# One layer of a hybrid encoder: parts of the FFN fronts, the projection's start, the scan's copies and the first output product moved to other places

## The chip, the cores and the metric

One core of one Trainium2 chip runs the whole layer as one program. The metric is the device time of one execution in microseconds (us), median of several executions. The engines are TensorE (PE, with its weight load PEld), VectorE (DVE), ScalarE (ACT), GpSimd (POOL) and SyncE (SP, which here only issues transfers). Each engine runs its own instructions in program order; semaphores order them against each other.

## What is computed

The reference is one layer on 1024 positions of width 1024 in float32, cut here to what matters.

```python
h = x
h = h + 0.5 * swiglu(rmsnorm(h, ffn1_norm), w_gate1, w_up1, w_down1)     # d_ff 2816
n = rmsnorm(h, mix_norm)
z = n @ w_in     # -> c_q 256 | c_kv 128 | k_rope 32 | u 512 | gate_attn 1024 | gate_ssm 1024
q  = rmsnorm(c_q, q_norm) @ w_uq         # 8 heads, 64 + 32 (rotary)
kv = rmsnorm(c_kv, kv_norm) @ w_ukv      # 8 heads, keys 64, values 64
attn = softmax(q k^T / sqrt(96)) v       # bidirectional, 8 heads
y = S5_forward(u) + S5_backward(u) + D*u # complex diagonal state, 32 groups, 64 states
g = gelu(y) @ w_glu + b_glu
ssm = g[:512] * sigmoid(g[512:])
h = h + (sigmoid(gate_attn) * (attn @ w_o_attn) + sigmoid(gate_ssm) * (ssm @ w_o_ssm)) @ w_out
h = h + 0.5 * swiglu(rmsnorm(h, ffn2_norm), w_gate2, w_up2, w_down2)
out = rmsnorm(h, final_norm)
```

## The kernel before

**Arithmetic.** Every float32 product is made of three passes on reduced operands: each operand is split in a high part (`hi`, a cast on ACT) and a rest (`lo`, a subtraction on DVE or POOL), and `three_passes` (L46) issues hi·hi, hi·lo and lo·hi into one PSUM tile (L48 to L50). So each operand tile goes raw, `high` (ACT), `low` (DVE or POOL), PE.

**Phases.** The program is a row of phases with a barrier of all engines between them (L69 is the instruction on which they wait): `ffn_phase` "f1", `project_phase`, `ssm_phase`, `mixer_phase`, `merge_phase`, `ffn_phase` "f2". `rows` holds the residual stream in SBUF, 8 tiles of 128 positions (ST = 8); KT = 8 slices of the width.

**FFN.** `ffn_phase` multiplies with seven products for each 2x2 block (A is the weight side, B the token side), q = 0 to 6. Blocks that are sums (`S`, made by `sums` on POOL, L1300) feed q = 1 and the other summed ones. At its front the eight tiles of `rows` are squared (L898, ACT), normalised in groups of two (`squares`, `normalised`; `Rstd`, L361), scaled (L1052, DVE), combined on POOL (L1282 to L1287) and turned on PE (L1314); `lows` are tiles 4 to 7, `sums` the combinations. The products begin in the order (block 0, q 0), (0, 2), (1, 0), (1, 2), then (0, 1), (0, 3) and so on; (0, 1) needs all four turned sums (`sums_high`, `sums_low`) and the operand `A_hi`, `A_lo` of block 1 (L933, L1036). In f2 the first raw weights and the gain are loaded by the merge before it; squares of tiles 0 to 3 are made there too.

**Projection.** `Norm` (L269) normalises and turns `rows` into `nT_hi`, `nT_lo`. Tiles 4 to 7 were scaled at the end of f1 and are turned at once, tiles 0 to 3 are squared, scaled (`pjn_xn`, L309) and turned after. `RowProduct` (L190, tag `rp`) then multiplies by 16 units of weights (two jobs of 448 and 512 columns, 8 slices each), with two weight slots: load, `high` (ACT, L230), `low` (DVE, L240), and 24 matmuls on PE over the 8 tiles of rows.

**SSM.** DVE runs a scan of 127 steps of three small operations (L1758, L1760, L1762). Beside it PE makes gate products: `Gates` (L1553, tag `ga`), one for each of 16 columns of 128, with two weight slots and two PSUM slots. For product n ACT reads the PSUM result of n with `sigmoid(n)` (L1587), which frees that slot for product n + 2, and then issues `high(n + 2)`; POOL makes `low(n + 2)` (L173). 13 products stand before the first output block (GATES_FIRST = 13), three between the blocks. `forward(b)` (L1703) copies the scan's states `ss_H` into `rows` with two copies on ACT (L1711); `forward(0)` waits for the semaphore of the last step of the scan (`act.wait_ge(s["scan"], CH)`). The output blocks on PE (L1683) wait for the copies.

**Mixer and merge.** The mixer makes the product with `w_glu` (`glu`, N = 8 products), turns the latents (`latent(m)`, 8 of them, one after each glu product), projects keys and queries of head 0 (`project(0, x)`), makes the product with `w_o_ssm` (`wos`, KT = 8) with one `value(m)` after each, and then the attention. The merge begins with `woa` (the product with `w_o_attn`, columns 0 to 7; the weights of the first 3 are loaded and split before), adds `gate` and `part` to it (L2466, L2469), multiplies by `w_out` and adds to `rows`, which it loads back as one transfer of 4 MB (`rows<-kept`, L2416). At the end f2 stores `rows` tile by tile to `kept` before it scales them.

Of the kernel before, what the change touches and what calls it, by code (L numbers as in the profile page):

```python
# [14 lines left out]
F32 = mybir.dt.float32  # L15
# [174 lines left out]
class RowProduct:  # L190

    def __init__(self, nc, ctx, tag, jobs, lhs, psum):
# [4 lines left out]
        self.raw = [sb(f"raw{i}", [P, HALF]) for i in range(2)]  # L199
        self.hi = sb("hi", [P, 2, HALF], F32R)  # L200
        self.lo = sb("lo", [P, 2, HALF], F32R)
        self.raw_in = [sem(f"raw_in{i}") for i in range(2)]
# [5 lines left out]
    def load(self, sp, n):  # L208
        units = self.units()
        w, parts, width = self.jobs[units[n][0]]  # L210
        k = units[n][1]
        if n >= 2:
            sp.wait_ge(self.lo_done, n - 1)
        for at, cols in parts:
            sp.dma_start(self.raw[n % 2][:, at:at + cols.stop - cols.start], w[k * P:(k + 1) * P, cols]).then_inc(self.raw_in[n % 2], 16)

    def arrived(self, n):

        units = self.units()
        return sum(16 * len(self.jobs[units[i][0]][1]) for i in range(n % 2, n + 1, 2))  # L220

    def high(self, act, n):
# [4 lines left out]
        act.wait_ge(self.raw_in[n % 2], self.arrived(n))  # L227
        if n >= 2:
            act.wait_ge(self.k_done, n - 1)
        act.copy(self.hi[:, n % 2, 0:width], self.raw[n % 2][:, 0:width]).then_inc(self.hi_done, 1)  # L230

    def low(self, eng, n):
# [5 lines left out]
        if n >= 2:  # L238
            eng.wait_ge(self.k_done, n - 1)
        eng.tensor_tensor(self.lo[:, n % 2, 0:width], self.raw[n % 2][:, 0:width], self.hi[:, n % 2, 0:width].bitcast(F32), ALU.subtract).then_inc(self.lo_done, 1)  # L240

    def products(self, pe, ready=None):

        units = self.units()
        for n, (j, k) in enumerate(units):
            if ready and j == 0:
                ready(k)
            w, parts, width = self.jobs[j]
            last = k == w.shape[0] // P - 1
            pe.wait_ge(self.lo_done, n + 1)  # L250
            for m in range(ST):
                if k == 0 and j:
                    pe.wait_ge(self.read, (j - 1) * ST + m + 1)
                hi, lo = self.lhs(j, k, m)
# [3 lines left out]
                elif last:  # L258
                    mm.then_inc(self.mm_done, 1)
# [2332 lines left out]
```

## Time and profile before

| | us |
|---|---|
| median of 3 runs (2269.16 to 2269.6) | 2269.32 |
| the profiled execution | 2267.31 |
| its span | 2265.5 |
| PE busy | 2144.2 |
| DVE busy | 1473.9 |
| ACT busy | 916.9 |
| POOL busy | 610.1 |

The profiled execution took 1.8 us more than its span, and the median is 2.0 us above it. Mean granted clock of TensorE was 0.982 of full speed. A row of the timeline gives start, length, engine, line, operation, output and inputs, count, and in brackets the idle time before it with what ended it. A row with a count spans several instructions in a row; its length is that of all of them.

### The profile page before, as it was taken

The page shows a single profiled execution, that of the slowest core. Times are in us where ns is not written, and L with a number is a line of the kernel's source. Part 1 is how long each engine was busy: PE and PEld are TensorE (multiplying, and loading weights), DVE is VectorE, ACT ScalarE, POOL GpSimd, SP SyncE. Part 2 cuts the span into 40 slices and gives each one's busy share as a digit, 9 for nine tenths or more (in the row PEclk, how much of TensorE's full clock was granted, in tenths as well). Part 3 has the DMA queues.
Part 4 walks back from the last instruction along what each step waited for, and adds up shares of the span by engine and source line. Part 5 has one row for each costly group of instructions (what it writes and reads, how often), then busy time and mean ns, then how long its engine had stood idle before and what let it go on. Part 6 is the DMA issues. An engine that isn't in the chain of part 4 may idle for free. (4 is left out here: it accounts for less than half of the span.)

```text
span 2265.5 us, 27670 instructions
## 1 busy us (share of the span) xinstructions
PE 2144.2 (95%) x10074; PEld 1779.3 (79%) x10074; DVE 1473.9 (65%) x2306; ACT 916.9 (40%) x1552; POOL 610.1 (27%) x510
## 2 busy tenths in 40 slices
PE   5899999999999899999999999899799999999997
PEld 4678888887887798878777887687678888887886
DVE  7786667657777524992447887454766565657777
ACT  5423333323445234225427778422533323324444
POOL 5337777750000003220002333100633333310000
PEclk9999999999999899999999999999899999999999
DMA  3433333349333427331340000362123232349333
GB/s 121 108 90 114 126 118 123 118 160 342 117 98 116 139 80 163 98 89 57 112 140 16 7 7 15 140 234 105 56 88 122 89 121 89 121 142 356 100 96 110
DMA packets 234471, 263.00 MB, mean 116 GB/s; under 512 B 34720, under 2 KB 169376, under 8 KB 233824
## 3 DMA queue, kind: packets, MB, share of 16 engines
q1 hardware_dynamic: 234336, 261.23, 36.4%
q8 instruction: 81, 1.33, 0.2%
q14 instruction: 54, 0.44, 0.1%
HBM read 184.60 MB, written 76.58 MB: 115 GB/s over the span
## 5 line engine op out<-in xcount | busy, mean ns | idle before, releaser
L48 PE MATMUL psum<-f_B_hi,f_A_hi 128*128 128x512 f32 x1232 | 489.8, 398 | 32.2 <-DVE f_A_lo L1036 23.7
L49 PE MATMUL psum<-f_B_lo,f_A_hi 128*128 128x512 f32 x1232 | 484.5, 393 | 0.0
L50 PE MATMUL psum<-f_B_hi,f_A_lo 128*128 128x512 f32 x1232 | 484.2, 393 | 0.0
L48 PEld LDWEIGHTS psum<-f_B_hi,f_A_hi 128*128 128x128 f32 x1232 | 234.2, 190 | 84.9 <-DVE f_A_lo L1036 27.5
L50 PEld LDWEIGHTS psum<-f_B_hi,f_A_lo 128*128 128x128 f32 x1232 | 234.2, 190 | 49.8
L49 PEld LDWEIGHTS psum<-f_B_lo,f_A_hi 128*128 128x128 f32 x1232 | 234.4, 190 | 47.6
L1300 POOL TENSOR_TENSOR f_S<-f_raw 128x512 f32<-128x512 f32 x88 | 134.7, 1531 | 445.5 <-DVE f_A_lo L1036 289.7
L933 ACT CAST f_A_hi<-f_S 128x512 fp32r<-128x512 f32 x176 | 109.2, 623 | 351.5 <-PE psum L50 347.1
L48 PE MATMUL psum<-f_wd,f_hh 128*128 128x512 f32 x616 | 240.4, 390 | 3.6 <-DVE f_wd L1082 3.6
L49 PE MATMUL psum<-f_wd,f_hh 128*128 128x512 f32 x616 | 240.4, 390 | 0.0
L50 PE MATMUL psum<-f_wd,f_hh 128*128 128x512 f32 x616 | 240.2, 390 | 0.0
L967 ACT CAST f_hh<-f_h_raw 128x512 fp32r<-128x512 f32 x154 | 96.0, 624 | 240.4 <-PE psum L50 231.7
L1036 DVE TENSOR_TENSOR f_A_lo<-f_raw,f_A_hi 128x512 fp32r<-128x512 f32 x132 | 132.4, 1004 | 70.1 <-ACT f_A_hi L933 69.4
L1080 DVE TENSOR_TENSOR f_hh<-f_h_raw,f_hh 128x512 fp32r<-128x512 f32 x154 | 106.6, 692 | 104.9 <-ACT f_hh L967 104.1
L1036 DVE TENSOR_TENSOR f_A_lo<-f_S,f_A_hi 128x512 fp32r<-128x512 f32 x176 | 138.7, 790 | 1.3 <-ACT f_A_hi L933 0.2
L933 ACT CAST f_A_hi<-f_raw 128x512 fp32r<-128x512 f32 x132 | 81.9, 620 | 142.1 <-PE psum L50 130.2
L48 PEld LDWEIGHTS psum<-f_wd,f_hh 128*128 128x128 f32 x616 | 116.0, 188 | 28.7 <-DVE f_wd L1082 4.4
L50 PEld LDWEIGHTS psum<-f_wd,f_hh 128*128 128x128 f32 x616 | 116.0, 188 | 24.2
L49 PEld LDWEIGHTS psum<-f_wd,f_hh 128*128 128x128 f32 x616 | 115.9, 188 | 23.9
L2211 DVE TENSOR_TENSOR mx_PT_lo<-psum,mx_PT_hi 128x512 fp32r<-128x512 f32 x128 | 87.8, 686 | 47.2 <-ACT mx_PT_hi L2076 46.8
L1737 POOL TENSOR_TENSOR u<-u,ss_C_mat 128x512 f32<-128x512 f32 x8 | 9.9, 1273 | 356.7 <-DMA ss_C_mat<-ssm_d 356.7
L1082 DVE TENSOR_TENSOR f_wd<-f_wd_raw,f_wd 128x512 fp32r<-128x512 f32 x154 | 105.7, 686 | 0.0
(327 smaller groups left out, 4277.3 us busy)
## 6 DMA issues: line engine op xcount, KB each, us to landing
f_h_raw<-hidden SPq DMA_DIRECT2D x154, 256.0 KB, 2.6
hidden<-rows SPq DMA_DIRECT2D x44, 768.0 KB, 4.6
f_raw<-ffn_w_gate SPq DMA_DIRECT2D x44, 512.0 KB, 5.1
f_raw<-ffn_w_up SPq DMA_DIRECT2D x44, 512.0 KB, 5.1
f_wd_raw<-ffn_w_down SPq DMA_DIRECT2D x44, 512.0 KB, 9.2
rows<-x SPq DMA_DIRECT2D x16, 512.0 KB, 7.3
ga_raw<-w_in SPq DMA_DIRECT2D x16, 512.0 KB, 4.3
gates<-ga_sig SPq DMA_DIRECT2D x32, 256.0 KB, 2.2
```

The lines of the kernel that those rows point to most:

```text
L48: pe.matmul(out, lhs_hi, rhs_hi, start=first, stop=False, skip_group_check=go_on)
L49: pe.matmul(out, lhs_hi, rhs_lo, start=False, stop=False, skip_group_check=go_on)
L50: return pe.matmul(out, lhs_lo, rhs_hi, start=False, stop=last, skip_group_check=go_on)
L933: act.copy(A_hi[:, q], src).then_inc(s_hi, 1)
L967: act.copy(hh[v % 2][0][:], h_raw[v % 8][:]).then_inc(s_dhi, 1)
L1036: eng.tensor_tensor(A_lo[:, q], src, A_hi[:, q].bitcast(F32), ALU.subtract).then_inc(s_lo, 1)
L1080: dve.tensor_tensor(hh[v % 2][1][:], h_raw[v % 8][:], hh[v % 2][0][:].bitcast(F32), ALU.subtract).then_inc(s_dlo, 1)
L1082: dve.tensor_tensor(wd[v % 2][1][:], wd_of(q, k), wd[v % 2][0][:].bitcast(F32), ALU.subtract).then_inc(s_dlo, 1)
L1300: pool.tensor_tensor(S[:, i], a, b, op).then_inc(s_sum, 1)
L1737: pool.tensor_tensor(u[:, g], u[:, g], Db[:, g].unsqueeze(2).broadcast_to([P, 4, T, SG]), ALU.mult).then_inc(s["ud"], 1)
L2211: dve.tensor_tensor(pt(PT_lo, g, x), turned_bank(x), pt(PT_hi, g, x).bitcast(F32), ALU.subtract).then_inc(s["tr_lo"], 1)
```

## The change

Six places are altered.

1. In both FFN fronts the operands of product (0, 1) are made before the turned sums (`high(0, 1)`, `low(0, 1)` now stand ahead of `sums_high` and `sums_low`).
2. Projection: four weight slots in `RowProduct` in place of two. PE turns tiles 4 to 7, then multiplies units 0 to 3 by these four tiles, with the turns of tiles 0 to 3 between the units, then the same units by tiles 0 to 3, then units 4 to 15 by all. Squares of tiles 0 to 2 are made at the end of f1 (on ACT). Only `square(3)` stays.
3. SSM: `forward(0)` and `forward(1)` stand after `sigmoid(8)` in place of after `sigmoid(11)`.
4. Mixer: after glu product 0 two latents are turned, then one after each; the same with the values after the wos products. On ACT and DVE the latents stand ahead of the glu's value and its split.
5. `woa.product(0)` moves from the start of the merge to the end of the mixer.
6. Merge and f2: in the merge SP stores tiles 4 to 7 of `rows` to `kept` after their additions, ACT squares tiles 4 to 6, POOL makes the first sums of weights (`next_S`). f2 squares only tile 7 and normalises tiles 4 to 7 as one group.

```diff
@@ RowProduct @@
+    S = 4
-        if n >= 2:
-            sp.wait_ge(self.lo_done, n - 1)
+        if n >= self.S:
+            sp.wait_ge(self.lo_done, n - self.S + 1)
...
+    def tiles(self, pe, n, ms, done):
...
+        pe.wait_ge(self.lo_done, n + 1)
+        for m in ms:
+            if k == 0 and j:
+                pe.wait_ge(self.read, (j - 1) * ST + m + 1)
+            hi, lo = self.lhs(j, k, m)
+            mm = three_passes(pe, self.psum[:, m, 0:width], hi, lo, self.hi[:, n % self.S, 0:width], self.lo[:, n % self.S, 0:width], k == 0, last)
+            if m == done:
+                mm.then_inc(self.k_done, 1)
...
@@ Norm @@
+        self.act_square(act, ST - self.AHEAD - 1)
         self.act_high(act, 0)
-        self.act_square(act, 0)
-        self.act_square(act, 1)
-        self.act_high(act, 1)
-        self.act_square(act, 2)
-        self.act_square(act, 3)
...
         newton(Chain(dve, self.s_rstd), st[:, 1, rest], st[:, 2, rest], st[:, 3, rest], st[:, 4, rest])
         dve.wait_ge(self.s_gain, 16)
         self.dve_rows(dve, 4)
+        for i in range(1, self.AHEAD):
+            self.dve_low(dve, i)
+        rp.low(dve, 0)
         self.dve_rows(dve, 5)
-        self.dve_low(dve, 2)
-        self.dve_low(dve, 3)
-        for i in range(4, ST):
+        rp.low(dve, 1)
+        for i in range(self.AHEAD, ST):
             self.dve_low(dve, i)
-            if i + 2 < ST:
+            if i < ST - 2:
                 self.dve_rows(dve, i + 2)
+                rp.low(dve, i - 2)
@@ project_phase, PE @@
-            for m in range(ST):
-                norm.pe(pe, m)
+            ahead, rest = norm.TILES[:norm.AHEAD], norm.TILES[norm.AHEAD:]
+            for i in range(norm.AHEAD):
+                norm.pe(pe, i)
+            for n in range(rp.S):
+                if n == 0:
+                    pe.wait_ge(norm.s_lo, norm.AHEAD)
+                rp.tiles(pe, n, ahead, rest[-1])
+                for i in ((4,), (5,), (6, 7), ())[n]:
+                    norm.pe(pe, i)
             pe.wait_ge(norm.s_lo, ST)
-            rp.products(pe)
+            for n in range(rp.S):
+                rp.tiles(pe, n, rest, rest[-1])
+            for n in range(rp.S, NU):
+                rp.tiles(pe, n, range(ST), ST - 1)
@@ ssm_phase, ACT @@
             for n in range(GATES_FIRST - 1):
                 side.sigmoid(act, n)
-            forward(0)
-            forward(1)
+                if n == GATES_FIRST - 5:
+                    forward(0)
+                    forward(1)
             side.sigmoid(act, GATES_FIRST - 1)
@@ mixer_phase @@
+        def sooner(n):
+
+            return (0, 1) if n == 0 else (n + 1,) if n + 1 < ST else ()
...
                 glu.product(pe, n, (lambda k: pe.wait_ge(s_lo, 2 * k + 2)) if n == 0 else None)
-                latent(n)
+                for m in sooner(n):
+                    latent(m)
...
+            pe.wait_ge(s["exp"], G)
+            woa.product(pe, 0, lambda k: pe.wait_ge(s["av_lo"], 4 * k + 4))
@@ merge_phase @@
-            sp.wait_ge(s_next, 64)
+            for i in range(QUAD):
+                sp.wait_ge(s_add, QUAD + i + 1)
+                sp.dma_start(kept[(QUAD + i) * P:(QUAD + i + 1) * P, :], rows[:, QUAD + i, :]).then_inc(s_keep[QUAD + i], 16)
...
+            for m in range(QUAD, ST - 1):
+                act.wait_ge(s_add, m + 1)
+                act.wait_ge(s_sq, m)
+                act.activation(dump[:], rows[:, m, :], ACT.Square, accum_out=next_stat[:, 0, m:m + 1]).then_inc(s_sq, 1)
...
-            for n in range(KT):
+            for n in range(1, KT):
                 woa.product(pe, n)
@@ ffn_phase, ACT and DVE at the front @@
+            if loaded:
+                square(ST - 1)
+                norm.root(act, 0, slice(QUAD, ST))
...
             high(1, 2)
+            high(0, 1)
             sums_high(0)
...
+            if loaded:
+                dve.wait_ge(s_sq, SQUARES)
+                norm.var(dve, 0, slice(QUAD, ST))
+                norm.inverse(dve, 0, slice(QUAD, ST))
+                scaled(QUAD)
+                scaled(QUAD + 1)
```

**The order on ACT in the SSM phase.** `ga_sig` is the result of a sigmoid, `ga_hi` the split weights for the product two later, `rows<-ss_H` the copies of `forward`. Before, near the end of the scan:

```order
539 L1587 ACTIVATE ga_sig<-psum 128x512 x2
540 L165 CAST ga_hi_8854<-ga_raw1 128x1024
541 L1711 COPY rows<-ss_H 64x128x8 x4
542 L1587 ACTIVATE ga_sig<-psum 128x512 x2
543 L165 CAST ga_hi_8854<-ga_raw0 128x1024
544 L1711 COPY rows<-ss_H 64x128x8 x2
```

After:

```order
537 L165 CAST ga_hi_8863<-ga_raw0 128x1024
538 L1752 COPY rows<-ss_H 64x128x8 x4
539 L1628 ACTIVATE ga_sig<-psum 128x512 x2
540 L165 CAST ga_hi_8863<-ga_raw1 128x1024
541 L1628 ACTIVATE ga_sig<-psum 128x512 x2
542 L165 CAST ga_hi_8863<-ga_raw0 128x1024
543 L1628 ACTIVATE ga_sig<-psum 128x512 x2
544 L165 CAST ga_hi_8863<-ga_raw1 128x1024
545 L1628 ACTIVATE ga_sig<-psum 128x512 x2
546 L165 CAST ga_hi_8863<-ga_raw0 128x1024
547 L1752 COPY rows<-ss_H 64x128x8 x2
```

The four copies, of which the first waits for the end of the scan, stood ahead of one sigmoid of the first 13; now they stand ahead of four of them.

**The order on PE at the start of the projection.** `rows` and `pjn_xn` are turned by the identity, `rp_hi` and `rp_lo` are the weights of the units. Before:

```order
2867 L357 MATMUL psum<-ident,rows 128x128 x32
2868 L357 MATMUL psum<-ident,pjn_xn 128x128 x32
2869 L48 MATMUL psum<-rp_hi,nT_hi 128x448
2870 L49 MATMUL psum<-rp_lo,nT_hi 128x448
2871 L50 MATMUL psum<-rp_hi,nT_lo 128x448
```

After, from the end of unit 0's part on tiles 4 to 7 (row 2867, the turns of tiles 4 to 7, is as before and the unit follows it at row 2868):

```order
2877 L48 MATMUL psum<-rp_hi,nT_hi 128x448
2878 L49 MATMUL psum<-rp_lo,nT_hi 128x448
2879 L50 MATMUL psum<-rp_hi,nT_lo 128x448
2880 L360 MATMUL psum<-ident,pjn_xn 128x128 x8
2881 L48 MATMUL psum<-rp_hi,nT_hi 128x448
2882 L49 MATMUL psum<-rp_lo,nT_hi 128x448
```

Twelve matmuls of a unit now stand between the turns of one tile and the next.

**The order on PE from the mixer to the merge.** `UNCONDITIONAL_BRANCH` marks the step from one phase to the next. Before:

```order
5373 L1987 MATMUL psum<-mx_PT_hi,mx_V 128x512
5374 L1988 MATMUL psum<-mx_PT_lo,mx_V 128x512
5375 L1792 UNCONDITIONAL_BRANCH
5376 L2497 UNCONDITIONAL_BRANCH
5377 L48 MATMUL psum<-aT_hi,woa_hi 128x512
```

After:

```order
5374 L2034 MATMUL psum<-mx_PT_lo,mx_V 128x512
5375 L2033 MATMUL psum<-mx_PT_hi,mx_V 128x512
5376 L2034 MATMUL psum<-mx_PT_lo,mx_V 128x512
5377 L48 MATMUL psum<-aT_hi,woa_hi 128x512
5378 L49 MATMUL psum<-aT_lo,woa_hi 128x512
```

The 24 matmuls of the first product now come before the branch.

## Rows read from the trace of the kernel before

**Rows 1.** Waits of PE, whole span: total us, times, longest.

```profile
PE psum L48 <- DVE f_A_lo L1036: 23.7, 6, 4.9
```

**Rows 2.** Windows, PE alone: stretch, length, PE busy (count), granted clock, DMA.

```profile
520.76:524.70 3.94, 3.94 (x10) 0.57 1.01 327
1451.14:1456.26 5.12, 5.12 (x12) 0.50 0.79 263
1477.00:1487.00 10.00, 10.00 (x46) 1.00 0.95 348
1586.53:1590.20 3.67, 3.67 (x32) 1.00 0.80 317
```

**Rows 3.** Timeline, first FFN's front, DVE and PE.

```profile
54.90 3.67 DVE L1070 TENSOR_TENSOR f_B_lo<-psum,f_B_hi 128x512 fp32r<-128x512 f32 x6
59.23 0.50 PE L48 MATMUL psum<-f_B_hi,f_A_hi 128*128 128x512 f32 x1 [2.87 <-DVE f_A_lo L1036]
```

**Rows 4.** Timeline, start of the projection: DVE, ACT and PE.

```profile
729.42 5.24 PE L357 MATMUL psum<-ident,rows 128*128 128x128 f32 x32 [2.77 <-PEq L69]
736.34 1.05 ACT L290 ACTIVATE u<-rows 128x1024 f32<-128x1024 f32 x1
738.96 2.48 DVE L309 SCALAR_TENSOR_TENSOR pjn_xn<-rows,pjn_stat,pjn_gb 128x1024 f32<-128x1024 f32 x2
751.19 1.23 DVE L325 TENSOR_TENSOR nT_lo<-psum,nT_hi 128x1024 fp32r<-128x1024 f32 x1 [0.82 <-ACT nT_hi L347]
753.09 0.70 PE L48 MATMUL psum<-rp_hi,nT_hi 128*128 128x448 f32 x1 [2.98 <-DVE rp_lo L240]
794.62 0.60 PE L48 MATMUL psum<-rp_hi,nT_hi 128*128 128x512 f32 x1 [1.28 <-ACT pj_zrow L1494]
```

**Rows 5.** Timeline, SSM phase: ACT, POOL, DVE and PE.

```profile
971.57 1.09 ACT L1587 ACTIVATE ga_sig<-psum 128x512 f32<-128x512 f32 x2 [8.86 <-PE psum L50]
982.45 1.09 ACT L1587 ACTIVATE ga_sig<-psum 128x512 f32<-128x512 f32 x2 [8.86 <-PE psum L50]
984.38 0.23 DVE L1760 TENSOR_TENSOR ss_H<-ss_H,ss_prod 128x64 f32<-128x64 f32 x1
984.55 2.39 POOL L173 TENSOR_TENSOR ga_lo<-ga_raw,ga_hi 128x1024 fp32r<-128x1024 f32 x1 [8.49 <-ACT ga_hi L165]
984.64 2.38 DVE L1762 TENSOR_TENSOR ss_H<-ss_H,ss_prod 128x64 f32<-128x64 f32 x1
1015.00 5.65 ACT L1711 COPY rows<-ss_H 64x1024 f32<-64x1024 f32 x3 [8.77 <-DVE ss_H L1762]
1018.92 1.45 PE L1683 MATMUL psum<-ss_C_mat,rows 128*128 128x128 f32 x7 [3.87 <-ACT rows L1711]
```

**Rows 6.** Timeline, PE in the mixer before the attention.

```profile
1132.47 0.79 PE L48 MATMUL psum<-mx_lT_hi,mx_w_hi 128*128 128x512 f32 x1 [4.21 <-DVE mx_lT_lo L2219]
1163.57 0.47 PE L48 MATMUL psum<-mx_sT_hi,wos_hi 128*128 128x512 f32 x1 [0.85 <-DVE mx_out L2265]
1189.83 0.47 PE L48 MATMUL psum<-mx_KT_hi,mx_QT_hi 96*128 96x512 f32 x1 [1.49 <-DVE mx_V L2223]
```

**Rows 7.** Timeline, end of the mixer and start of the merge.

```profile
1448.65 1.26 POOL L2330 TENSOR_TENSOR aT_lo<-mx_att,aT_hi 64x512 fp32r<-64x512 f32 x1 [0.81 <-ACT aT_hi L2107]
1451.14 0.77 PE L48 MATMUL psum<-aT_hi,woa_hi 128*128 128x512 f32 x1 [6.12 <-PEq L69]
1473.63 1.23 DVE L2466 TENSOR_TENSOR mg_val<-psum,mg_gate 128x1024 f32<-128x1024 f32 x1 [4.72 <-DMA mg_gate<-gates]
```

**Rows 8.** DMA issues from 1450 to 1475: operation, count, KB, us to landing.

```profile
rows<-kept SPq DMA_DIRECT2D x1, 4096.0 KB, 17.9
```

**Rows 9.** Timeline, second FFN's front, PE and DVE.

```profile
1601.27 1.20 DVE L100 TENSOR_TENSOR f_stat<-f_stat 128x2 f32<-128x2 f32 x1
1610.29 0.79 PE L48 MATMUL psum<-f_B_hi,f_A_hi 128*128 128x512 f32 x1 [4.35 <-DVE f_A_lo L1036]
1627.45 0.80 PE L48 MATMUL psum<-f_B_hi,f_A_hi 128*128 128x512 f32 x1 [2.87 <-DVE f_A_lo L1036]
```

More of the change, by code:

```diff
@@ L760, in ffn_phase @@
         s_gain, s_sq, s_xn, s_T, s_tr, s_bhi, s_blo = map(sem, ("gain", "sq", "xn", "T", "tr", "bhi", "blo"))
-        s_kept = [sem(f"kept{m}") for m in range(ST if x is None else 0)]
+        if loaded:
+            ctx.taken += loaded[4].taken
+        s_kept = loaded[5] if loaded else None
+        SQUARES = 1 if loaded else ST
         s_raw = [sem(f"raw_in{j}") for j in range(2)]
@@ L987, in _ @@
             first_copy(0)
-            squares(3)
+            if not loaded:
+                squares(3)
             high(1, 0)
             high(1, 2)
+            high(0, 1)
             sums_high(0)
@@ L1025, in _ @@
                     last.root(act, 0, FGROUPS[0])
+            if following:
+                for m in range(QUAD - 1):
+                    act.wait_ge(s_o11, QUAD + m + 1)
+                    act.wait_ge(s_o12, QUAD + m + 1)
+                    act.wait_ge(s_fsq, QUAD + m)
+                    act.activation(fdump[:], rows[:, m, :], ACT.Square, accum_out=following[2][:, 0, m:m + 1]).then_inc(s_fsq, 1)
             if finish:
@@ L2025, in _ @@
                 wos.product(pe, n, (lambda k: pe.wait_ge(s_vlo, k + 1)) if n == 0 else None)
-                value(n)
+                for m in sooner(n):
+                    value(m)
             for g in range(G + LAG + 2):
@@ L2150, in _ @@
                         queries(0, x)
-                value(n)
+                for m in sooner(n):
+                    value(m)
             split(1)
@@ L2266, in _ @@
                 wos.low(dve, n + 3)
-                value(n)
+                for m in sooner(n):
+                    value(m)
                 if n == 1:
@@ L2552, in build @@
         where, _ = ffn_map(-(-nc.sbuf_base // 32) * 32)
+        stores = Taken()
         loaded = ([nc.alloc_sbuf_tensor_at(f"f2_raw{j}", [P, KT, 2 * P], F32, offset=where["raw"] + 8 * 1024 * j) for j in range(2)],
[L2554 removed]
+                  nc.alloc_sbuf_tensor_at("f2_gb", [P, D], F32, offset=where["ring"]),
+                  nc.alloc_sbuf_tensor_at("f2_S", [P, 4, KH, P], F32, offset=where["S"]),
+                  nc.alloc_sbuf_tensor_at("f2_stat", [P, 5, ST], F32, offset=where["stat"]),
+                  stores, [semaphores(nc, stores, "keep")(f"tile{m}") for m in range(ST)])
         merge_phase(nc, w, psum, rows, kept, woa, held, loaded, gates, partial, w["ffn2_norm"][0])
```

188 lines of the change are left out of this document (102 added, 86 removed).

## The prediction

> **What bounds the kernel now.** I read the page's busy times first: PE works 2144 of 2265.5 us, so only its idle stretches and its slow stretches can be won or lost. Then the waits of PE by releaser: the dearest, 23.7 us in six, is on `f_A_lo` at the FFN fronts [rows 1]. Then each wait of PE at its place in the timeline. The changed places hold these: 2.87 in the first front [rows 3], 2.77, 5.64, 2.11 and 2.98 at the projection's start (the first and last of them in [rows 4]), 3.87 at the first SSM output block [rows 5], 4.21, 0.85 and 1.49 in the mixer [rows 6], 6.12 at the merge [rows 7], and in the second front 4.91, 4.35 and 2.87 (the last two in [rows 9]). Last, the granted clock behind them. After 6.12 idle, 12 matmuls took 5.12 us at 0.50 (the 1.2 GHz level), 0.427 each; later 46 took 10.00 at 1.00 (2.4 GHz), 0.217 to 0.227 [rows 2]. So a long wait costs 1.3 to 2.5 more behind it. A wait of 2.19 left the clock at 1.00, yet one of 1.79 was followed by 0.57 [rows 2]: short waits are uncertain, those of 2.8 and more were always followed by the slow level.
>
> **The change, part by part** (minus saves; all against the profiled execution, 2267.3 us).
>
> *First front.* PE stood from 56.36 to 59.23 for `A_lo` of (0, 1), which DVE made behind the last turned sums; those end at 58.57 [rows 3]. With `A_lo` made earlier, PE needs the fourth of the last five, one operation of 0.61 earlier: 58.0. That is 1.2, and the wait shrinks to 1.6, so the slow stretch behind it (1.7) goes: **-2.9**. If the clock falls all the same, -1.2; if DVE also hands the sums over later because of the two operations moved ahead of them, -0.5. Range -3 to -0.5.
>
> *Projection.* Costs first. Three squares of 1.05 and their read of 0.19 [rows 4] go to the end of the first FFN, where ACT would do them one after another behind the last additions, which end at 728.0; the last ends near 730.0 and the barrier opens about 2.0 later than now (from 0 if ACT kept up fully, to 3.7 if all three stood behind the end). From that start: PE turns tiles 4 to 7 in 5.24 [rows 4]. One square, a high part and the small operations (0.2 each) put the first scaled row at 4.5 us after the turns begin on DVE, then DVE makes one row (1.24), three lows (1.2 each) and one unit's low (0.6): unit 0 begins 10.6 after the first turn, at 740.0 on the old scale, PE having waited 5.3. Its 12 matmuls run at the slow level, 0.375 each, 4.5. Then follow turns, 12 matmuls, turns and so on, up to 756.4, when the last low is there (now 752.4 [rows 4]; later since DVE has the units' lows in between). What is left of the first four units, 48 matmuls of 0.20, ends at 766.0. Before, these 96 began at 753.09, nine of them slow: 9 x 0.375 + 87 x 0.20 = 20.8, so 773.9. That is -7.9. Add +2.0 for the late start, +0.5 for turns at the slow level, -1.28 for the wait at 794.62 [rows 4], since with four slots ACT no longer sits behind a slot before it empties PSUM: **-6.7**, range -8.5 to -4. The 4 MB load of E comes at its old time, behind the same turns, and has 8 us of cover.
>
> *SSM, the largest term.* `forward(0)` waits for the last step of the scan, and ACT takes its work in order. Now it is issued after `sigmoid(11)` (1004.2) and its wait is 8.77 long, over at 1015.00 [rows 5]. Moved behind `sigmoid(8)` (971.57), it holds ACT from about 973.6 to the scan's end, and behind it are queued `sigmoid(9)` to `(12)` and the splits for products 11 to 14. PE runs product 10 (its weights were split behind sigmoid 8), which ends at 993.2, since a product ends every 10.88, as the two sigmoids show [rows 5]. Product 11 needs weights split behind sigmoid 9 and the PSUM slot that sigmoid 9 frees, so PE stops. The scan gains a little: while POOL subtracts (2.39) one small DVE operation takes 2.38 in place of 0.23 [rows 5]; this happens 11 times, and the last three (from 984.55 on) no longer fall into the scan: 3 x 2.14 = 6.4. So it ends at 1008.6. Four copies (7.2, from 5.65 for three [rows 5], overlapped) end at 1015.8, sigmoid 9 at 1016.8, its split at 1017.8, POOL's low 2.4 later at 1020.2. PE has stood 27.0. Product 11 costs 10.88 and 2.3 for the slow level, product 12 10.88: the first output block starts at 1044.2, now 1018.92 with 1.7 of slow clock behind it [rows 5]: **+23.6**. If the scan gained nothing it would be +30; if the low-clock stretch is small and the copies are quicker, +21.
>
> *Mixer.* Keys begin right behind the last glu product: the wait of 4.21 [rows 6] and 1.5 of slow clock go, -5.7. But what the queries and the wos products need comes by ACT, DVE and a transfer, and moves up by less, about 3.7. So the wait of 0.85 at the fifth wos product [rows 6] grows to some 2.5. The values made one earlier take away the 1.49 at 1189.83 [rows 6] and 0.3 more: -5.7 + 2.0 - 1.8 = **-5.5**, range -6.5 to -3.5 (where the wait of 2.5 is followed by the slow level).
>
> *First output product in the mixer.* Meant to fill the 6.12 before the merge [rows 7]. Its last six matmuls need POOL's `aT_lo`, which ends at 1449.91 [rows 7], so it ends near 1451.4 and the barrier opens 1.35 later. It would save 24 x 0.227 + 2.5 of slow clock - 1.35 = 6.6. But the next thing late is a transfer: DVE waited 4.72 for `gate(2)` until 1473.63 [rows 7], queued behind the 4 MB of `rows`, which took 17.9 [rows 8], with the DMA engines full. Product 4 needs the PSUM slot that this step frees at 1474.9, and it began at 1475.4, with no slack. All transfers start 1.35 later, so product 4 begins at 1476.2 at the earliest, PE having stood 7.3 and being slow for 2.0 more: 0.8 + 2.0 = **+2.8**, range 0 to +4.
>
> The Trainium skill (DMA: Bandwidth & Descriptors, Queues, rings and completion order) says that what one engine issues shares one ring on each DMA engine, and there descriptors are taken in order, so a small transfer issued behind a large one cannot pass it. It speaks against this move: by it the term is +2.8, without it -6.6. The 4.72 of the trace agrees.
>
> *Merge and second front.* The additions' stores of tiles 4 to 7 and the squares go into the merge (barrier +0.5, since the last store is issued after the last addition), POOL's first sums as well. In f2 one normalisation of four tiles replaces two of two. The second one is what holds DVE from 1598.64 to 1604.99: its small operations take 1.20 beside POOL where they take 0.16 alone [rows 9]. It goes, and the first starts two squares earlier. (0, 2) comes 1.3 sooner, (1, 0) 5.7 sooner, and (0, 1), now at 1627.45 [rows 9], has its sums about 8.2 sooner; one slow stretch (1.3) goes. +0.5 - 8.2 - 1.3 = **-9.0**, range -11 to -6 (what POOL still has to combine, 16 operations of 1.3 to 1.7, becomes the limit).
>
> **Sum.** -2.9 - 6.7 + 23.6 - 5.5 + 2.8 - 9.0 = +2.3: 2269.6 for the profiled execution. The median of the runs is 2.0 above it: **2272**.
>
> **Rivals.**
> *Slower: the projection's start stays at the slow clock.* DVE must make for every turned tile a low (1.2), a row (1.24) and a unit's low (0.6), 3.0 in all, against some 3.4 of PE work. If each piece ends with a wait long enough, the 48 matmuls of the first pass all take 0.375 and not 0.20, 36 more slow ones than I counted: +6.3, 2278. For: the four waits there are now 2.1 to 5.6 long, and the first nine matmuls behind them still took 0.375. Against: more PE work between them. It decides once PE waits between units are of 2 us and more.
> *Faster: the first output product pays in full.* If the transfers issued 1.35 later land no later, because PE's traffic is not what fills them, product 4 waits for nothing new: -6.6 in place of +2.8, 2262.5. Against it stands the 4.72 of [rows 7].
> *The copies don't hold ACT.* If the wait were met before the end of the scan, the SSM term would fall to about -2 and the sum to -23: 2246. Against: the wait of 8.77 ended with the last scan operation [rows 5], and the semaphore's value is unchanged.
>
> **How the numbers follow.** Forecast 0.68, its own range 2266 to 2277 (the terms' ranges, each reaching 1.5 to 2.5 either way, taken together). Slow projection 0.17, product in full 0.11, copies free 0.04. Measurement can tell 0.2% from no change, 4.5 us: 2264.8 to 2273.9. Of the forecast's 0.68, 0.45 lie inside, 0.20 above, 0.03 below. So faster 0.03 + 0.11 + 0.04 = 0.18, same 0.45, slower 0.20 + 0.17 = 0.37. The range takes in the slow rival and most of the fast one: 2263 to 2279.
>
> **What would show it.** On PE one wait of some 27 us from 993, on ACT one of about 35 before the first `rows<-ss_H`, and 8 collisions in the scan where there were 11; no wait at 59 over 1.7; the first unit at about 10.6 after the first turn; no wait ahead of the keys, a larger one at the fifth wos product; product 4 of the merge waiting 7 us for DVE behind `gate(2)`; the second front's (0, 1) about 33 us after its start. I am wrong if ACT's wait is short, if the scan ends near 1015 all the same, or if the merge's first transfers land earlier than now.

## The result and the profile after

The changed kernel takes 2278.03 us (median of 7 runs, 2276.15 to 2281.39) against 2269.6 (median of 7, 2269.13 to 2271.57): ratio 1.0037, 95% interval 1.0026 to 1.0048. It is 8.4 us slower, inside the range of 2263 to 2279, 6 above the 2272 that I named. Its profiled execution, at 2281.39, is the slowest of its seven, so the trace shows 3.4 us more than the median. The profiled execution of the kernel before (2267.31) is faster than each of its runs listed with the changed kernel (2269.13 and up). So the two traces lie further apart than the two medians; where the difference lies is told below.

The waits of PE, by releaser (total us, times, longest), show two that are new. Before, the dearest was `f_A_lo` with 23.7 in six [rows 1].

```profile
PE psum L48 <- POOL ga_lo L173: 23.4, 1, 23.4
PE psum L48 <- DVE f_A_lo L1053: 12.9, 3, 4.8
PE psum L48 <- DVE mg_val L2539: 7.7, 1, 7.7
```

**The SSM phase.** The timeline of ACT, POOL and PE (start, length, instruction, idle before and what ended it), which answers to [rows 5]:

```profile
964.20 1.09 ACT L1628 ACTIVATE ga_sig<-psum 128x512 f32<-128x512 f32 x2 [9.22 <-PE psum L50]
998.40 7.34 ACT L1752 COPY rows<-ss_H 64x1024 f32<-64x1024 f32 x4 [32.17 <-DVE ss_H L1804]
1005.55 1.09 ACT L1628 ACTIVATE ga_sig<-psum 128x512 f32<-128x512 f32 x2
1007.65 2.34 POOL L173 TENSOR_TENSOR ga_lo<-ga_raw,ga_hi 128x1024 fp32r<-128x1024 f32 x1 [38.96 <-ACT ga_hi L165]
1010.05 0.79 PE L48 MATMUL psum<-nT_hi,ga_hi 128*128 128x512 f32 x1 [23.40 <-POOL ga_lo L173]
```

ACT issues sigmoid 8 at 964.20, then waits 32.17 us for the last step of the scan. The four copies take 7.34. Only then come sigmoid 9, the split, POOL's low, and PE begins product 11 after 23.40 of nothing. Each link of the prediction is there, and both waits are some 3 to 4 shorter than it said (about 35 on ACT, 27 on PE). The scan ran from 873.80 to 998.37, 124.6 long and with 8 of its operations held beside POOL; before it was 130.9 with 11, as forecast.

**The fronts, the projection, the mixer.** PE, in the order of the places of [rows 3, 4, 6]:

```profile
57.95 0.47 PE L48 MATMUL psum<-f_B_hi,f_A_hi 128*128 128x512 f32 x1 [1.76 <-DVE f_B_lo L1087]
62.65 0.47 PE L48 MATMUL psum<-f_B_hi,f_A_hi 128*128 128x512 f32 x1 [1.69 <-DVE rows L1149]
...
727.78 5.85 PE L360 MATMUL psum<-ident,rows 128*128 128x128 f32 x32 [4.71 <-PEq L69]
738.30 0.71 PE L48 MATMUL psum<-rp_hi,nT_hi 128*128 128x448 f32 x1 [4.67 <-DVE rp_lo L242]
747.86 0.47 PE L48 MATMUL psum<-rp_hi,nT_hi 128*128 128x448 f32 x1 [0.79 <-DVE rp_lo L242]
...
1175.86 0.66 PE L48 MATMUL psum<-mx_sT_hi,wos_hi 128*128 128x512 f32 x1 [2.50 <-DVE mx_out L2316]
```

The wait for (0, 1) went from 2.87 to 1.76, and the next one, for DVE, grew from 0.93 to 1.69. The barrier before the projection costs 1.94 more (4.71 for 2.77), and the first unit begins 10.52 after the first turn. The wait at the fifth wos product grew from 0.85 to 2.50.

**The merge.** The windows of PE (stretch, length, busy and count, granted clock, DMA share, GB/s), DVE and PE in the timeline, and the transfer of `rows` (count, KB, us to landing), to hold beside [rows 7, 8]:

```profile
1466.50:1483.11 16.61, 16.60 (x72) 1.00 0.94 354
1483.11:1490.84 7.73, 0.00 (x1) 0.73 1.04 397
...
1489.47 1.22 DVE L2539 TENSOR_TENSOR mg_val<-psum,mg_gate 128x1024 f32<-128x1024 f32 x1 [9.37 <-DMA mg_gate<-gates]
1490.84 0.77 PE L48 MATMUL psum<-aT_hi,woa_hi 128*128 128x512 f32 x1 [7.73 <-DVE mg_val L2539]
...
rows<-kept SPq DMA_DIRECT2D x1, 4096.0 KB, 18.8
```

PE does products 1 to 3 without a break (72 matmuls), then stands 7.73 while the DMA engines are full. DVE's wait for `gate(2)`, 4.72 before, is 9.37. SP issues the 4 MB of `rows` and then `gate(2)`. In the kernel before:

```profile
1454.02 0.54 SPq L2416 DMA_DIRECT2D rows<-kept  x1
1461.77 0.33 SPq L2412 DMA_DIRECT2D mg_gate<-gates  x1
```

and in the changed kernel:

```profile
1469.33 1.08 SPq L2468 DMA_DIRECT2D rows<-kept  x1
1472.75 1.65 SPq L2464 DMA_DIRECT2D mg_gate<-gates  x1
```

The 4 MB land 17.9 and 18.8 us after their issue, at about 1471.9 and 1488.1. DVE goes on with `gate(2)` at 1473.63 and 1489.47, 1.7 and 1.4 behind that, though `gate(2)` was issued 7.8 behind the 4 MB in one case and 3.4 in the other.

**The second front.** PE, to hold beside [rows 9]:

```profile
1605.67 5.35 PE L1343 MATMUL psum<-ident,rows 128*128 128x128 f32 x32 [2.94 <-PEq L69]
1617.64 0.80 PE L48 MATMUL psum<-f_B_hi,f_A_hi 128*128 128x512 f32 x1 [3.87 <-DVE f_A_lo L1053]
1640.32 0.47 PE L48 MATMUL psum<-f_B_hi,f_A_hi 128*128 128x512 f32 x1 [1.19 <-DVE f_B_lo L1087]
1645.01 0.47 PE L48 MATMUL psum<-f_B_hi,f_A_hi 128*128 128x512 f32 x1 [1.69 <-DVE rows L1149]
```

The wait of 4.35 in the middle is gone, and (0, 1) comes 34.65 after the start; before it was 40.92. The last of POOL's 16 combinations ends at 1638.42, just ahead of PE's last turns:

```profile
1637.15 1.27 POOL L1315 TENSOR_TENSOR f_T_A_hi<-rows,f_T_A_hi 128x512 f32<-128x512 f32 x1
```

**Where the time went.** Each stretch is the distance between two instructions of PE that both timelines have; the last column is what I had forecast for it.

| stretch of PE | before | changed | difference | forecast |
|---|---|---|---|---|
| first turn to last product of the first FFN | 715.00 | 711.31 | -3.7 | -2.9 |
| barrier | 2.77 | 4.71 | +1.9 | +2.0 |
| projection | 114.06 | 105.15 | -8.9 | -8.7 |
| SSM phase, to the mixer's first turn | 228.75 | 254.80 | +26.1 | +23.6 |
| mixer, to the first turn of `mx_prob` | 127.57 | 124.27 | -3.3 | -5.5 |
| attention | 240.82 | 240.85 | 0.0 | 0 |
| end of the mixer and merge | 143.72 | 149.88 | +6.2 | +2.8 |
| barrier | 2.19 | 2.94 | +0.8 | +0.5 |
| second front | 61.65 | 54.77 | -6.9 | -9.5 |
| the rest | 617.32 | 618.86 | +1.5 | 0 |
| sum, with 0.1 before the first turn | | | +13.8 | +2.3 |

The 13.8 is the difference of the two spans (2279.3 and 2265.5). About 5 of it (1.5, 1.6 and 1.9) is not in every trace of the same code, most of it slow clock. After the same wait of 1.8 us (2059.62 here, 2047.38 before) the clock fell this time, and not in the trace of before:

```profile
2059.62:2063.90 4.28, 4.28 (x12) 0.60 1.05 395
```

That is the +1.5 of "the rest". The turns at 1605.67 took 5.35, partly at the low level, and 3.72 before, 1.6. The stretch of the end of the mixer and the merge is 149.88 here and 148.02 in e1 below, which has the same merge, 1.9 less: PE's wait for DVE is 7.26 there for 7.73, and the rest is a shorter slow stretch behind it. The first FFN has it the other way: of its -3.7, 1.5 is a slow stretch in the trace of before only [rows 2]. With all four off, the trace says 13.8 - 5.0 + 1.5 = 10.3; the medians say 8.4, 5.9 to 10.9 by the interval.

### The profile page after: what moved, and what is told of

Same layout as the page of the kernel before. It is cut to its first block and busy times, and to the rows that moved or that the text cites. A ratio compares the mean times of both kernels' runs of the same rounds, so it can differ in the third digit from the quotient of the medians.

```text
span 2279.3 us, 27668 instructions
## 1 busy us (share of the span) xinstructions
PE 2150.0 (94%) x10074; PEld 1778.2 (78%) x10074; DVE 1468.7 (64%) x2300; ACT 918.1 (40%) x1551; POOL 611.4 (27%) x510
## 5 line engine op out<-in xcount | busy, mean ns | idle before, releaser
L1328 POOL TENSOR_TENSOR f_S<-f_raw 128x512 f32<-128x512 f32 x86 | 129.9, 1511 | 304.4 <-DVE f_A_lo L1053 284.2
L1097 DVE TENSOR_TENSOR f_hh<-f_h_raw,f_hh 128x512 fp32r<-128x512 f32 x154 | 106.6, 692 | 105.0 <-ACT f_hh L973 104.1
L48 PE MATMUL psum<-nT_hi,ga_hi 128*128 128x512 f32 x256 | 103.1, 403 | 24.2 <-POOL ga_lo L173 23.4
```

The source lines that it names most:

```text
L48: pe.matmul(out, lhs_hi, rhs_hi, start=first, stop=False, skip_group_check=go_on)
L1097: dve.tensor_tensor(hh[v % 2][1][:], h_raw[v % 8][:], hh[v % 2][0][:].bitcast(F32), ALU.subtract).then_inc(s_dlo, 1)
L1328: pool.tensor_tensor(S[:, i], a, b, op).then_inc(s_sum, 1)
```

## The experiments

Times are medians; "before" is the kernel before, measured beside each. Its median lies between 2269.6 and 2273.5, so kernels that had different medians of it beside them are compared by their ratio to it. 0.1% is 2.3 us.

| kernel | us | before | ratio, 95% interval |
|---|---|---|---|
| changed | 2278.03 | 2269.60 | 1.0037, 1.0026 to 1.0048 |
| e1 copies back | 2250.64 | 2273.51 | 0.9901, 0.9888 to 0.9915 |
| e2 changed, 32 bytes of padding | 2277.55 | 2273.51 | 1.0022, 1.0013 to 1.0030 |
| e3 before, 160 bytes of padding | 2269.97 | 2273.51 | 0.9988, 0.9980 to 0.9997 |
| e4 changed, product back in the merge | 2275.09 | 2273.51 | 1.0007, 0.9998 to 1.0016 |
| e6 e1 with nT on a multiple of 128 bytes | 2253.67 | 2270.55 | 0.9922, 0.9907 to 0.9937 |
| e7 e1 with rows loaded two steps later | 2251.47 | 2270.55 | 0.9913, 0.9898 to 0.9928 |
| e8 before with the copies moved | 2293.82 | 2270.55 | 1.0100, 1.0083 to 1.0116 |
| e9 before with the mixer's order | 2264.18 | 2270.55 | 0.9967, 0.9954 to 0.9980 |
| e10 e1 with rows loaded behind gate 5 | 2244.41 | 2269.72 | 0.9890, 0.9877 to 0.9904 |
| e11 e10 with the product back | 2251.69 | 2269.72 | 0.9922, 0.9908 to 0.9935 |
| e12 before with the fronts' order | 2266.95 | 2269.72 | 0.9989, 0.9980 to 0.9998 |
| e13 e1 with rows loaded behind gate 7 | 2244.33 | 2269.79 | 0.9888, 0.9871 to 0.9904 |

### The copies: undone (e1), and alone (e8)

```diff
             for n in range(GATES_FIRST - 1):
                 side.sigmoid(act, n)
-                if n == GATES_FIRST - 5:
-                    forward(0)
-                    forward(1)
+            forward(0)
+            forward(1)
```

> The changed kernel with forward(0) and forward(1) back behind sigmoid(11), all else as changed. If the copies hold ACT and so PE (my account: a wait of 23.4 us before product 11, its slow clock 2.3, less the 3.9 that stood before the first output block and its 1.7, i.e. about -20 to -24), the time is 2278 - 22 = 2256, and PE's wait of 23.4 is gone. If the copies cost nothing themselves and the phase is late for another reason (the gate products, 11.24 us apart where they were 10.88), it stays within 5 us of 2278.

e8 makes the opposite edit in the kernel before.

> The kernel before with forward(0) and forward(1) behind sigmoid(8), nothing else. My account: PE waits 27.2 for product 11 (gate products are 10.88 apart here), the scan ends 6.4 sooner, the first output block starts 25.3 later and its slow clock of 1.7 goes: +23.6, 2293 against 2269.6. If the copies cost what the changed kernel lost in this phase (26.1) for another reason than the slower matmuls, +26.

e1 takes 2250.64, 26.9 less than e2, which has the changed kernel's order and was measured beside the same runs of before. That is more than the 20 to 24 that I had expected of e1: I had counted the old wait of 3.9 before the first output block and its 1.7 of slow clock as coming back, and they did not (told under the 160 bytes). In e1's trace the SSM phase's stretch from the second gate product to the mixer is 187.7 long; it was 188.1 before and 213.8 in the changed kernel. e8 is 23.3 slower than before (22.7 by the ratio). Its timeline, ACT and PE:

```profile
1007.54 7.35 ACT L1711 COPY rows<-ss_H 64x1024 f32<-64x1024 f32 x4 [34.97 <-DVE ss_H L1763]
...
1019.21 0.80 PE L48 MATMUL psum<-nT_hi,ga_hi 128*128 128x512 f32 x1 [26.92 <-POOL ga_lo L173]
```

ACT waits 34.97 (forecast about 35), PE 26.92 (27.0), and the whole costs 23.3 (23.6). The scan runs from 883.05 to 1007.54, 6.5 shorter than before. In the kernel before, three of POOL's splits fell into its last part and each held one DVE operation 2.15 longer; here they don't. The Trainium skill (SBUF — State Buffer, Who interferes with whom) says that a VectorE instruction with two inputs in SBUF contends with a GpSimd instruction that reads SBUF, over a port pair that the two share and that is an exclusive lock. Both kinds are of this form here, and the 6.5 agrees with three such holds; the traces with the copies moved (changed, e2, e4, e8) have 8 of them in the scan, all others 11. So the account is shown from both sides: the copies hold ACT, ACT holds PE, and this one edit turned the gain of the rest into a loss.

### The 160 bytes: slower matmuls (e3, e2, e6)

In the changed kernel the gate products stand 11.24 apart and no longer 10.88. The windows of PE over 80 us of these products (length, busy and count, clock) for the kernel before:

```profile
900.00:980.00 80.00, 80.00 (x355) 1.00 0.37 106
```

and for the changed kernel:

```profile
900.00:980.00 80.00, 80.00 (x343) 1.00 0.30 86
```

That is 0.225 and 0.233 a matmul at the same granted clock; from the spacing of whole products of 48, 10.88 and 11.24, it is 0.2267 and 0.234. One thing that the prediction had passed over could do this: the new tensor `carry` holds 160 bytes of each partition and moves everything allocated behind it, nT_hi and nT_lo among it.

```diff
         ident = ctx.enter_context(nc.sbuf_tensor("ident", [P, P], F32))
+        ctx.enter_context(nc.sbuf_tensor("pad", [P, 40], F32))        # e3, in the kernel before
```

> The kernel before with 160 unused bytes a partition behind the identity, nothing else. Theory address: gate products at 0.2343 a matmul in place of 0.2267, 11.24 apart; 768 x 0.0076 = 5.8 and some 2 more in the projection's first units, but the scan hides part of the first 13 products (PE waited 3.87 for it): 2269.6 + 3 to +7 = 2273 to 2277. Rival (order): no change, 2269 to 2271.

e2 has 32 bytes more behind `carry`, e6 96 bytes ahead of nT_hi (with the copies back):

```diff
+        ctx.enter_context(nc.sbuf_tensor("pad", [P, 8], F32))         # e2
...
             with ExitStack() as inner:
+                inner.enter_context(nc.sbuf_tensor("pad_n", [P, 24], F32))   # e6
                 nT_hi, nT_lo = ...
```

> The changed kernel with 32 bytes of padding a partition behind the new tensor of statistics (160 bytes), so that everything allocated after it starts on a multiple of 64 bytes as it did before the change. Theory address: the gate products are slower (0.2343 us a matmul, 0.2267 before) because the 160 bytes moved nT_hi and nT_lo to an address 32 bytes off a multiple of 64. Then the matmuls go back to 0.2267, 768 x 0.0076 = 5.8 us less in them; while PE waits for the copies anyway, 480 of those matmuls come before the wait, and a scan of fixed length hides their gain, so only those behind it count: 288 x 0.0076 = 2.2, with 1 us more in the projection: 2275. Rival, the slower matmuls come from the order (other engines at the same time): 0.2343 stays, 2278.

> Copies back behind sigmoid(11), and 96 unused bytes a partition ahead of nT_hi, so that nT begins on a multiple of 128 bytes, as in the kernel before (66176 there; 66336 in the changed kernel, 32 over a multiple of 128; with 32 bytes of padding 66368, 64 over). Theory: the gate products take 0.2343 us a matmul whenever the moved operand nT begins off a multiple of 128 bytes. Then 0.2267 comes back and the three products between the output blocks give 144 x 0.0076 = 1.1 us: about 1 below the kernel with the copies back. Rival: the place of nT matters not, what was moved is something else of the 160 bytes (the identity's neighbours, u, the projection's tiles): 0.2343 stays.

The same window in e3:

```profile
900.00:980.00 80.00, 80.00 (x344) 1.00 0.35 102
```

in e2:

```profile
900.00:980.00 80.00, 80.00 (x344) 1.00 0.28 81
```

and in e6:

```profile
900.00:980.00 80.00, 80.00 (x354) 1.00 0.32 93
```

The kernel before becomes slow in these products by 160 unused bytes alone, so no order of work is the cause. 32 bytes of padding don't mend it, as I had expected them to: my first rule, multiples of 64 bytes, is wrong. With nT_hi at 66432, a multiple of 128, the full rate is back. All four placements tried fit "multiples of 128 bytes": 66176 and 66432 are fast, 66336 and 66368 slow. Both fast ones are odd multiples of 128, so that a coarser rule holds is not excluded.

But e3 is no slower than the kernel before (0.9988), against my +3 to +7, and e6 no faster than e1. PE had waited 3.87 for the end of the scan at the first output block. The slower products fill just that wait (12 x 0.36 = 4.3), and the clock does not fall behind it. The first output block in e1, whose products are slow:

```profile
1008.88 3.77 PE L1724 MATMUL psum<-ss_C_mat,rows 128*128 128x128 f32 x32
```

and in e6, whose products are fast:

```profile
1007.44 5.44 PE L1724 MATMUL psum<-ss_C_mat,rows 128*128 128x128 f32 x32 [3.90 <-ACT rows L1752]
```

e6 waits 3.90 and then pays 1.67 of slow clock, more than the 1.1 that the three later gate products give back. In the changed kernel, where the copies make the wait, the slower rate is not free: products 11 to 15 lose 5 x 0.36 = 1.8.

### The first output product (e4, e7, e10, e11, e13)

e4 undoes the move:

```diff
-            pe.wait_ge(s["exp"], G)
-            woa.product(pe, 0, lambda k: pe.wait_ge(s["av_lo"], 4 * k + 4))
...
-            for n in range(1, KT):
+            for n in range(KT):
                 woa.product(pe, n)
```

> The changed kernel with woa.product(0) back at the start of the merge. My account: moved forward it filled a wait but the transfers behind it start later and PE then waits 7.7 for the gate's; in the trace this stretch lost about 5 to 6 us against the kernel before. So back in its place it gives 2278 - 5 = 2273, and the wait of 7.7 at the fourth product is gone. Rival: the transfers' lateness has nothing to do with the move (for instance the stores or the SP queue), then the time rises by 6 to 2284 and the wait stays.

It is 2.5 faster than e2, measured beside the same runs of before (by the ratios 3.4 against e2, 6.8 against the changed kernel; I had expected 5). From the attention's last products to the end of the merge its trace has 145.1, e1's, with the product in the mixer, 148.0: the move costs 2.9. DVE's step for `gate(2)` in e4:

```profile
1488.22 1.23 DVE L2537 TENSOR_TENSOR mg_val<-psum,mg_gate 128x1024 f32<-128x1024 f32 x1 [4.26 <-DMA mg_gate<-gates]
```

It waits 4.26, as the kernel before did (4.72), and PE no longer waits for it. Now the load that stands in front, with the product kept in the mixer and the copies back. Two steps later (e7):

```diff
                 woa.load(sp, n + AHEAD)
-                if n == 1:
-                    sp.dma_start(rows[:], ...).then_inc(s_kept, 16)
                 if n == 3:
                     load(sp, 0)
                     load(sp, 1)
+                    sp.dma_start(rows[:], ...).then_inc(s_kept, 16)
```

> Copies back behind sigmoid(11), the first output product kept in the mixer, and in the merge the 4 MB load of rows issued two steps later, behind the first loads of w_out. My account of the merge: PE's wait of 7.3 at the fourth product is for gate(2), queued behind these 4 MB. Then the wait goes and its slow clock (2.2) too: 9 us below the kernel with the copies back, and 6 below one with the product in its old place. Rival: the engines' DMA rate, not the order in the queue, is the limit (the same bytes are needed by then anyway): the wait only moves, and the gain is under 2.

Behind the first, DVE waits at most 0.45 for the next three gates, and the fifth pays: DVE and PE in e7,

```profile
1472.43 1.23 DVE L2537 TENSOR_TENSOR mg_val<-psum,mg_gate 128x1024 f32<-128x1024 f32 x1 [11.01 <-DMA mg_gate<-gates]
1473.80 0.76 PE L48 MATMUL psum<-aT_hi,woa_hi 128*128 128x512 f32 x1 [5.76 <-DVE mg_val L2537]
```

A wait of 5.76 in place of 7.26 in e1: 1 us gained in this stretch where I had expected 9, as the rival had it, and it left open whether order or rate is the limit. e10 puts the load behind the sixth gate (`if n == 5`), e13 behind the eighth (`if n == KT - 1`).

> Copies back behind sigmoid(11), the first output product kept in the mixer, the 4 MB load of rows issued behind the sixth gate, some 25 us later than in the changed kernel. Issuing it two steps later only moved PE's wait (5.8 in place of 7.3, for the fifth gate). If the wait is for the bytes ahead in the queue, none of the early gates has them ahead now: the wait and its slow clock go, and this stretch gains 9 us on the kernel with the copies back (rows are needed for the first addition, some 85 us after the merge's start). If gates, parts and weights alone fill the DMA engines, a wait of 3 or more stays at one of the products 4 to 6, and the gain is under 4.

> The best kernel so far (copies back, product in the mixer, rows loaded behind the sixth gate) with that load behind the eighth and last gate. There PE still waited 2.5 at the first product with w_out, for DVE behind gate(6), and gates 6 and 7 were issued behind the 4 MB. If it is the queue's order, that wait goes: 2 to 2.5 less, 2242. If rows then come too late for the first addition (some 60 us after), DVE waits there and the time rises; I expect not.

In e10 no wait is left at products 2 to 7, and one of 2.50 at the first product with `w_out`; in e13 that one is 0.91:

```profile
1487.80 0.50 PE L48 MATMUL psum<-mg_wo_hi,mg_mT_hi 128*128 128x512 f32 x1 [2.50 <-DVE mg_val L2538]
```

```profile
1490.26 0.47 PE L48 MATMUL psum<-mg_wo_hi,mg_mT_hi 128*128 128x512 f32 x1 [0.91 <-DVE mg_wo_lo L2445]
```

From the merge's first product to the second FFN's first turn: e1 137.3, e7 136.3, e10 132.8, e13 129.5. So e10 gains 4.5 here on e1, half of the 9 expected, since one wait moved on to the product with `w_out`. e10 is 2244.41, a ratio of 0.9890; e1's is 0.9901, and the intervals of the two overlap. e13, 3.2 shorter in this stretch, has the same median (2244.33, ratio 0.9888); the two intervals are 6 and 7.5 us wide, and its trace shows the turns behind it at 5.35, the slow level. Whether e13 is better stays open. The gates were late because they stood behind 4 MB in one queue: the same bytes, issued behind the last gate, hold none of them. The Trainium skill (DMA: Bandwidth & Descriptors, Queues, rings and completion order) has the rule, descriptors are consumed in ring order on each DMA engine; it adds that a later descriptor's write may even so finish before an earlier one's, so that a small transfer "cannot pass" is the prediction's conclusion and not the page's sentence. The traces agree with the order: PE's wait behind a gate stands before product 4 in e1 (7.26), before product 6 in e7 (5.76), before the first product with `w_out` in e10 (2.50), and in e13 nowhere. That the queue's order does it, and not the DMA engines being full with the 4 MB, rests on this and on `gate(2)` landing right behind the 4 MB in both traces above. No run sent the gates by another queue.

e11 is e10 with the product back in the merge.

> As the run before it, with woa.product(0) back at the start of the merge. The load's place should then matter nothing (in the changed kernel with the product back no wait of more than 1.2 stood there), so this is 6 to 7 us above the run with the product in the mixer if the move's gain of 6.6, as I worked it out, exists once no transfer eats it. Rival: both the same, the product in the mixer brings nothing even then.

2251.69 against 2244.41, measured beside the same runs of before: 7.3 more, and every run of e11 is slower than every run of e10. So the move pays once the load is out of its way, and the 6.6 that I had worked out is within what the medians allow. The size is less sure: from the attention's last products to the end of the merge the two traces are 148.7 and 144.9, 3.8 apart, and e10 lost some 1.5 more than e1 to slow clock at the end of the attention.

### The mixer's order and the fronts' order, each alone (e9, e12)

```diff
-                latent(n)
+                for m in sooner(n):
+                    latent(m)
```

e9 is the kernel before with this, the same for the values, and the two latents on ACT and DVE moved ahead.

> The kernel before with the latents and values one product earlier (point 4 of the change), nothing else. I had put it at -5.5; in the changed kernel's trace the stretch is 3.4 to 3.5 shorter: -3.5. If the stretch gained less only because of its surroundings there, -5.5.

PE's wait at the fifth wos product in e9:

```profile
1157.24 0.76 PE L48 MATMUL psum<-mx_sT_hi,wos_hi 128*128 128x512 f32 x1 [2.66 <-DVE mx_out L2272]
```

From the first glu product to the keys of head 1, the stretch is 106.6 (110.4 before, 106.9 in e1): -3.9. The matmul behind the wait is 0.76 long, the slow level's length; it is 0.47 at the fast one [rows 6]. In e6, e7 and e13, which have the same order, the clock stayed up behind this wait:

```profile
1151.37 0.47 PE L48 MATMUL psum<-mx_sT_hi,wos_hi 128*128 128x512 f32 x1 [2.48 <-DVE mx_out L2315]
```

This is e7, and there the stretch is 105.4, 5.0 less than before. The whole kernel gains more than the 3.5 expected, 0.33% (0.20 to 0.46%), 4.5 to 10 us; its profiled execution is only 2.6 below that of before, which was itself below all other runs of before. I have not found what the rest is, if it is anything.

e12 has `high(0, 1)` and `low(0, 1)` ahead of the turned sums:

> The kernel before with high(0, 1) and low(0, 1) ahead of the turned sums in both FFN fronts (point 1 of the change), nothing else. I had put it at -2.9 for the first front (1.2 of waiting, 1.7 of slow clock); traces of the changed kernel show the wait at 1.7 and the next one, behind DVE, grown from 0.93 to 1.69, so -1.5 to -2.9 there. In the second front the same edit alone should give up to the same, so -3 to -5 in all: 2265 to 2267 against 2269.6. If POOL's contention with the moved operations eats it, 0.

PE at the two fronts in e12:

```profile
57.33 0.47 PE L48 MATMUL psum<-f_B_hi,f_A_hi 128*128 128x512 f32 x1 [1.76 <-DVE f_B_lo L1071]
...
1626.32 0.47 PE L48 MATMUL psum<-f_B_hi,f_A_hi 128*128 128x512 f32 x1 [1.76 <-DVE f_B_lo L1071]
```

Both waits went from 2.87 to 1.76. The kernel is 0.11% faster (0.02 to 0.20%), 2.8 us by the medians, just under the 3 to 5 expected. That both fronts gain can't be told from one alone at this size.

## Why the prediction was right, and where its sizes were off

**Direction and mechanisms.** All six terms had the right sign. The SSM term, on which the whole hung, is shown by e1 and e8, link by link. The time is 6 above the one named, which lies in three terms: the SSM phase (2.5), the mixer (2.2) and the second front (1.5 to 2.6). That it lies inside the range is in part luck: it is 1 above the forecast's own range of 2266 to 2277, and the whole range reached 2279 for the sake of the slow projection, a rival that did not come about.

**The SSM term, +26.1 for +23.6.** In the kernel before, the edit alone costs 23.3, as worked out. What I missed is a line of the change that the diff ahead of the prediction leaves out: `carry`, a new tensor of 160 bytes ahead of everything. It makes gate products 0.36 longer; product 10 ends 3.7 later after the scan's start than I put it, so that PE's wait is 23.4 and not 27.0, and product 11 begins 136.2 after the scan's start, as worked out. So the first ten cost nothing; from there products 11 to 15 lose 1.8 of the 2.5. The step that failed is "a product ends every 10.88", taken over without asking where its operand lies.

**The mixer, -3.3 for -5.5.** The wait at the fifth wos product is 2.50, as forecast, and the keys start at once. But the slow clock came back behind the new wait of 2.5, so that the 1.5 of slow clock won at the keys was lost again: the range's end "where the wait of 2.5 is followed by the slow level" is what happened (-3.5). In e6, e7 and e13 the clock stayed up there, and the same stretch gained 5.0 to 5.2. The prediction called short waits uncertain, and then the sum took the favourable side.

**The first product, +2.9 for +2.8,** by e4 against e1. The profiled execution shows 6.2 for the whole stretch: the rest is 1.4 that e4 also has (before its first merge product, 1.5 of slow clock at the end of the attention, which the trace of before lacks) and 1.9 that e1 does not have. The rival that it pays in full was wrong here, and near as a statement of what the move is worth without the load in its way: e11 against e10 gives 7.3 by the medians, 3.8 in the traces' stretch.

**The second front, -6.9 to -8 for -9.5** (e1 -8.0 with the turns at full clock, the changed kernel -6.9). I had (0, 1) at 32.7 after the start. It came at 33.5 in e1 and 34.7 in the changed kernel: POOL's 16 combinations take 24.9 in all, from 1613.5, and run up to 1638.4, just before PE's last turns, as the end "16 operations of 1.3 to 1.7" of the range had it.

**The first front and the projection** came as forecast: -3.7 for -2.9 (of which 1.5 is a slow stretch that the trace of before has after its 1.79 wait and this one not), and -7.0 with its barrier for -6.7. The rival of a projection at the slow clock did not come about: between the units PE waited at most 0.79, and the granted clock was 1.00 from 743 on.

**The chances.** I gave "slower" 0.37 and "same" 0.45, so the less likely of the two came. With +1.8 for the address the forecast alone would have stood on the edge, and the slow clock behind waits near 2 us I had counted as gone where it sometimes comes back. A sum made of losses and gains of 24 each is as good as its worst term.

**A better kernel** came out: e10, 2244.41, 1.1% below the kernel before, is five of the six edits with the copies where they were and the load of `rows` issued later. Most of that is e1, the copies put back; what the later load adds to the whole time (0.1%) is not clear of noise.

## What to carry to other kernels

Before you move an instruction forward on an in-order engine, look at what it waits for, not at what it needs room for: one wait for the end of a 130 us chain, set three products too early, stopped the engine whose work feeds PE, and cost more than all the other edits won. When you fill a barrier's wait with work, look at the queue that starts at the barrier: if a large transfer stands ahead of small ones there, move it first, and then the filled wait can pay (e10 against e11). And a new tensor, however small, moves all that is allocated behind it: look at its size modulo 128 bytes, which is the step that all four placements here fit.

## What the runs showed of the hardware

- Matmuls of 512 columns whose moved operand lay at 66336 or 66368 in a partition took 0.2343 us; at 66176 and 66432, both multiples of 128 bytes, 0.2267 (e3, e2, e6), all at a granted clock of 1.00. e6 shows that the cause is among nT_hi, nT_lo and what is allocated behind them; it does not tell which of these.
- A slower engine can be free or better: the 4.3 us lost in 12 products filled a wait of 3.87 and kept the clock up, and the kernel was not slower (e3 0.9988, 0.9980 to 0.9997).
- After waits of 1.8 us TensorE's clock fell in some executions and not in others in a stage that no edit touched (at 2047.38 before it stayed, at 2059.62 in the changed kernel it fell, 1.5 us), which is as much as some of the terms of the sum.
- The same holds for longer waits. Behind 2.38 to 2.48 at the fifth wos product the granted clock was 1.00 in e6, e7 and e13; behind 2.29 to 2.66 at the same place it was 0.63 to 0.70 over the next 5 us in the changed kernel, e1, e2, e4, e9, e10 and e11. Behind 2.94 at the second front's barrier the 32 turns took 3.68 to 3.69 at 1.00 in e1, e2, e4, e6 and e10, and 5.35 at 0.68 in the changed kernel, e7, e11 and e13. So the prediction's "2.8 and more always" holds for the trace it was read from, and not for these.
- While POOL subtracted (2.39), one operation of the scan on DVE took 2.3 to 2.5 in place of 0.23 to 0.29, and the scan was 6.2 to 6.5 us shorter with 8 such meetings than with 11.
